# The sample's keys and values in two buffers each, its steps and heads re-spaced, and the output matrix loaded in eight pieces, in a streaming encoder step

## The chip, the cores and the metric

The kernel runs on one core of a Trainium2 chip. The metric is the device time of one execution in microseconds (us), smaller is better. TensorE (PE; PEld is its weight load), VectorE (DVE), ScalarE (ACT) and GpSimd (POOL) compute. SyncE (SP) computes nothing: it issues DMAs and waits. GpSimd issues the indirect DMAs. Each engine works through its own list in order.

## The reference

One layer for a prompt of 1024 tokens and a sample of 32 tokens that has 2048 tokens of cached keys and values. After one joint projection come stick-breaking attention, window attention, the output matrix, and a retrieval network (PEER) that fetches, for each token and each of 8 heads, 16 rows out of 16384.

```python
def stick_breaking(q, k, v, q_pos, k_pos):
    z = jnp.einsum('bqhd,bshd->bhqs', q, k).astype(jnp.float32) * (HEAD_DIM ** -0.5)
    visible = (k_pos[None, :] < q_pos[:, None])[None, None]
    log_keep = jnp.where(visible, jax.nn.log_sigmoid(-z), 0.0)
    between = lax.cumsum(log_keep, axis=3, reverse=True) - log_keep
    a = jnp.where(visible, jnp.exp(jax.nn.log_sigmoid(z) + between), 0.0)
    return jnp.einsum('bhqs,bshd->bqhd', a.astype(v.dtype), v)
...
    merged = jnp.concatenate([rms_norm(o_sb.reshape(b, t, SB_WIDTH), g_sb),
                              rms_norm(o_sw.reshape(b, t, SWA_WIDTH), g_sw)], axis=-1)
    h = x + merged @ w_out
    return h + peer_ffn(rms_norm(h, g_ffn), w_q, keys_1, keys_2, u, v)
...
        # peer_ffn: scores against two sets of 128 keys, top 16 of each, top 16 of their sums -> ids, gs
        hid = jax.nn.gelu(jnp.einsum('thkd,td->thk', u[ids], xs), approximate=False)
        return jnp.einsum('thk,thkd->td', gs * hid, v[ids])
```

## The kernel before, in words

A first phase projects the first 384 prompt tokens and the sample. The second phase, `fused_phase`, takes nearly all of the time. Its backbone is 1056 **gathers**: `pool.indirect_dma_start` (L895) fetches 128 rows of `peer_uv`, 8 KB each (1.05 MB), into one of 7 buffers `uv`; DVE takes their dot product with the tokens (`dot`, L1112), ACT makes a gelu of it and a diagonal matrix (`experts`, L1033 and L1039), and PE adds the weighted rows up (`experts`, L1627, two gathers at a time). A buffer is free again after that matmul: POOL waits for it (`vmm`) before the gather 7 places on.

All engines run the same loop over **slots** n; slot n has gather n. Everything else is hung on slots by hand, through functions that give a slot number; engines run ahead of one another as far as semaphores let them. There are 8 prompt tiles t of 128 tokens, and the sample is t = 8 (`NT`). For each, in order:

- **steps** (`step_slot`): 2 to 16 of them for a prompt tile, 17 for the sample, each over 128 keys. For a step at slot n, SP loads keys (`load_k`) and values (`load_v`), PE makes `scores` at n into `z`, ACT `softplus` at n + 1, DVE `keep` at n + 3, PE `sums` at n + 4, ACT `weights` at n + 6, PE `values` at n + 8. Steps of prompt tiles stand 4 slots apart and have two buffers for keys and two for values; the sample's stand 5 apart (slots 822 to 902), with one buffer each. So `load_k` of a sample step holds for the scores of the step ahead, and `load_v` for its values.
- the window (four slots, 4 apart), the tail (norms, output matrix, residual), and
- eight **heads** (`route_slot`), at slot n: PE makes `queries` (L1564) in slots n and n + 1, DVE cuts the scores at n + 9 (`first_eight`, whose L1239 frees the bank that the next head's queries wait for, `cut`), and the row numbers are there at n + 18. Heads stand 11 slots apart in tile 1, 14 or 15 in tiles 2 to 7, and 9 in the sample (slots 961 to 1024).

ACT's `log_table()` loads the table set for exp and ln before `softplus` and before `weights` where the last set was another; the gelu in `experts`, which runs in odd slots, loads its own again. The output matrix `w_out` (4.2 MB) for tiles 3 to 8 goes into the space of the late projection's buffers: `load_w_out` (L812) issues four DMAs of 1 MB at slot 222, ahead of the first keys of tile 3, whose first step is at slot 229.

## Time and profile before

| | |
|---|---|
| median of 3 runs | 3384.24 us (3364.96 to 3384.81) |
| the profiled execution's own time | 3389.14 us |
| its span, first to last instruction | 3387.3 us |
| busy: PE, DVE, ACT, POOL | 2562.7, 2221.3, 1388.7, 1601.4 us |
| mean granted clock of PE | 0.882 of full |
| read from HBM | 1201.97 MB |

The span leaves out 1.8 us of the execution's own time, and the profiled execution took 4.9 us more than the median run. The DMA share of a stretch is the busy time of the 16 DMA engines' packets over that of the stretch; where packets of two queues overlap it reads slightly above 1.

### The profile page before, as it was taken

How to read it: one execution, taken by the hardware profiler on the slowest of the kernel's cores; microseconds unless marked ns; L12 is line 12 of the kernel's file. 1: busy time of each engine (PE TensorE's matmuls, PEld its weight loads, DVE VectorE, ACT ScalarE, POOL GpSimd, SP SyncE). 2: the span in 40 equal slices, each digit the busy share in tenths (PEclk: the TensorE clock that was granted, in tenths of full speed). 3: DMA queues.
4: the chain of work that ended last, by engine and by line, in shares of the span. 5: the costliest groups of instructions: out<-in, count | busy, mean ns of one | idle time of the engine just before them, and what ended most of it. 6: DMA issues, size and time to landing. Idle time of an engine off the chain costs nothing.

```text
span 3387.3 us, 38329 instructions
## 1 busy us (share of the span) xinstructions
PE 2562.7 (76%) x10637; PEld 1201.1 (35%) x10637; DVE 2221.3 (66%) x5640; ACT 1388.7 (41%) x3224; POOL 1601.4 (47%) x1634
## 2 busy tenths in 40 slices
PE   7898787877858676877787768876887777767664
PEld 4464333433324322432343224332343234322321
DVE  2037746785657857776777666777777666675775
ACT  2124522652226424652365335544565344442222
POOL 1104444443535555555555544555554554456443
PEclk9899889988979888979799889888998888888777
DMA  6538899999989999999999999999999999999887
GB/s 213 175 97 327 329 407 416 375 381 349 421 354 391 380 381 401 371 381 396 381 387 363 383 397 357 378 384 406 363 395 387 406 391 383 377 393 390 354 355 291
DMA packets 246919, 1225.21 MB, mean 362 GB/s; under 512 B 30721, under 2 KB 90801, under 8 KB 110513
## 3 DMA queue, kind: packets, MB, share of 16 engines
q0 software_dynamic: 154208, 1112.07, 82.3%
q1 hardware_dynamic: 92496, 110.69, 10.0%
q8 instruction: 85, 1.39, 0.2%
q14 instruction: 130, 1.06, 0.1%
HBM read 1201.97 MB, written 20.79 MB: 361 GB/s over the span
## 4 chain that ended last, share of the span: by engine, by line
PE 37%; DMA 26%; DVE 10%; issue 7%; ACT 6%; POOL 5%; DVEq 2%; ACTq 1%; SPq 1%; POOLq 0%
DMA f_uv<-peer_uv,f_idx 18%; PE f_y_acc L1627 17%; PE f_q_ps L1564 5%; DVE f_uv L1112 4%; DMA f_work<-cache_sb_kT 4%; POOL f_uv L895 3%; PE f_z L1523 3%; PE f_z L1390 2%; DMA f_work<-scratch_projT 2%; ACT f_diag L1039 2%; ACT L1033 2%; PE f_z L1371 2%; POOL f_gate_fold L883 1%; PE f_z L1397 1%; PE f_o_sb L1416 1%
## 5 line engine op out<-in xcount | busy, mean ns | idle before, releaser
L895 POOL DMA_INDIRECT f_uv<-peer_uv,f_idx x1056 | 1244.9, 1179 | 1625.9 <-PE f_y_acc L1627 1338.0
L1112 DVE CUSTOM_DVE_ANT_0 f_uv<-f_uv,f_x_rep 128x1024 f32<-128x1024 f32 x1056 | 1304.0, 1238 | 779.7 <-DMA f_uv<-peer_uv,f_idx 777.1
L1627 PE MATMUL f_y_acc<-f_uv,f_diag 128*64 128x512 f32 x4224 | 1249.9, 712 | 578.6 <-ACT f_diag L1039 562.1
L1627 PEld LDWEIGHTS f_y_acc<-f_uv,f_diag 128*64 128x64 f32 x4224 | 300.1, 154 | 1198.1 <-ACT f_diag L1039 726.0
L1033 ACT ACTIVATE f_act_hid<-f_hid 128x2 f32<-128x2 f32 x528 | 107.2, 203 | 1272.7 <-DVE f_hid L1112 1270.5
L1564 PE MATMUL f_q_ps<-r_w_q,f_xnT 128*128 128x256 f32 x1152 | 311.1, 421 | 55.1 <-DVE f_cut L1239 55.1
L883 POOL TENSOR_TENSOR f_gate_fold<-r_fold,f_gates 128x128 f32<-128x128 f32 x528 | 328.6, 622 | 9.7
L1039 ACT ACTIVATE f_diag<-f_gate_fold,f_act_hid 128x64 f32<-128x64 f32 x1056 | 310.3, 340 | 37.9 <-issue 1.1
L1564 PEld LDWEIGHTS f_q_ps<-r_w_q,f_xnT 128*128 128x128 f32 x1152 | 233.2, 210 | 141.3 <-DVE f_cut L1239 65.2
L1033 ACT ACT_TABLE_LOAD x196 | 251.5, 1283 | 3.5
L908 ACT ACT_TABLE_LOAD x119 | 152.7, 1283 | 240.7 <-PE f_z L1371 189.7
L1390 PE MATMUL f_z<-f_work,r_neg_suffix 128*128 128x512 f32 (+2 forms) x178 | 105.1, 676 | 10.5 <-DVE f_work L1134 5.9
L367 PE MATMUL proj<-xnT,w_cols 128*128 128x416 f32 x288 | 106.4, 526 | 2.7 <-DVE xnT L332 2.7
L1523 PE MATMUL f_z<-r_w_out,f_work 128*128 128x512 f32 (+1 forms) x192 | 93.9, 625 | 10.2 <-DVE f_work L1199 10.2
L1371 PE MATMUL f_z<-f_q_pad,f_work 128*128 128x256 f32 x288 | 79.6, 401 | 28.3 <-DMA f_work<-scratch_projT 28.3
L1416 PEld LDWEIGHTS f_o_sb<-f_work 128*128 128x128 f32 (+2 forms) x848 | 91.4, 166 | 26.0 <-issue 21.2
L1134 DVE SCALAR_TENSOR_TENSOR f_work<-f_z,f_work 128x512 f32<-128x512 f32 (+2 forms) x89 | 56.9, 640 | 54.1 <-ACT f_work L929 49.1
L1416 PE MATMUL f_o_sb<-f_work 128*128 128x64 f32 (+2 forms) x848 | 91.6, 255 | 0.4 <-DMA f_work<-cache_sb_v 0.2
L1112 DVE DVE_READ_ACCUMULATOR2_ANT f_hid<- 128x1 f32 x1056 | 85.7, 81 | 0.0
L1371 PEld LDWEIGHTS f_z<-f_q_pad,f_work 128*128 128x128 f32 x288 | 57.1, 201 | 72.7 <-issue 67.9
L1491 PE MATMUL f_o_sb<-r_w_out 128*128 128x256 f32 (+1 forms) x224 | 72.6, 444 | 0.0
L367 PEld LDWEIGHTS proj<-xnT,w_cols 128*128 128x128 f32 x288 | 55.2, 196 | 46.4 <-issue 43.1
(184 smaller groups left out, 2747.1 us busy)
## 6 DMA issues: line engine op xcount, KB each, us to landing
f_uv<-peer_uv,f_idx POOLq DMA_INDIRECT x1056, 9.5
f_work<-scratch_projT SPq DMA_DIRECT2D x86, 128.0 KB
w_cols<-w_blocks SPq DMA_DIRECT2D x18, 512.0 KB, 3.9
r_w_out<-w_blocks SPq DMA_DIRECT2D x36, 256.0 KB, 7.2
f_work<-out_sb_v_prompt SPq DMA_DIRECT2D x72, 128.0 KB, 7.3
r_w_q<-w_peer_q SPq DMA_DIRECT2D x8, 1024.0 KB, 7.5
x_in<-x_prompt SPq DMA_DIRECT2D x8, 512.0 KB, 4.6
f_q_pad<-scratch_projT SPq DMA_DIRECT2D x64, 64.0 KB
```

The lines of the kernel that those rows point to most:

```text
L367: last = nc.tensor.matmul(acc[c % 2][:, 0:EARLY + TS], w[:, c % 2, k, :], xnT[:, k, :], start=(k == 0), stop=(k == DK - 1))
L883: nc.gpsimd.tensor_tensor(gate_fold[:, batch % 4, :, :], fold[:].unsqueeze(1).broadcast_to(full), gates[:, t % 2, head, k:k + 2].unsqueeze ...
L895: pool.indirect_dma_start(uv[:, n % RING, :], None, io["peer_uv"], bass.IndirectOffsetOnAxis(ap=idx[:, t % 2, head, k:k + 1], axis=0),).th ...
L1033: nc.scalar.activation(act_hid[:, batch % 4, :], hid[:, batch % 8, :], ACT.Gelu)
L1039: made = nc.scalar.activation(diag[:, batch % 3, i, :], gate_fold[:, batch % 4, i, :], ACT.Copy, scale=act_hid[:, batch % 4, i:i + 1])
L1112: nc.vector.tensor_tensor_reduce(row_u, row_u, x_rep[:, g % 2, :], 1.0, 0.0, ALU.mult, ALU.add, hid[:, n // 2 % 8, n % 2:n % 2 + 1]).then_ ...
L1371: last = nc.tensor.matmul(z[:, at:at + 256], kT[:, (e % 2) * 256 + m * P:(e % 2) * 256 + (m + 1) * P], q_pad[:, f, m, :, :].rearrange("p a ...
L1390: nc.tensor.matmul(out, neg_suffix[0:keys, 0:keys], sp[0:keys, 0:width], start=False, stop=False, skip_group_check=True)
L1416: last = nc.tensor.matmul(o_sb[0:n, hd * HD:(hd + 1) * HD], probs[0:keys, i * n:(i + 1) * n], v_blk[0:keys, col:col + HD], start=(e == 0 a ...
L1523: last = nc.tensor.matmul(z[0:rows, b * 512:(b + 1) * 512], mergedT[:, k, 0:rows], w[:, b * 512:(b + 1) * 512], start=(k == 0), stop=(k == ...
L1564: last = nc.tensor.matmul(q_ps[:, 0:2 * QH], xnT[:, k, :], w_q[:, k, head * 2 * QH:(head + 1) * 2 * QH], start=(k == 0), stop=(k == DK - 1))
L1627: last = nc.tensor.matmul(y_acc[i * GT:(i + 1) * GT, b * 512:(b + 1) * 512], diag[:, batch % 3, i, :], uv[:, n % RING, DM + b * 512:DM + ( ...
```

## The change

The sample's steps stand 4 slots apart in place of 5: they still begin at slot 822 and end at 886 in place of 902. Its window moves from slot 913 to 896, its tail from 933 to 916, and its heads stand 11 slots apart, at 944 to 1021 in place of 961 to 1024. Keys and values of odd steps get second buffers, `k_odd` and `v_odd`, in halves of attention buffers that the sample's narrower steps leave free; each lies there in two runs of 1 KB a partition. The cached keys are laid out in memory so that a partition's 512 numbers are one run of 2 KB, where they were four of 512 B. The output matrix is loaded in eight pieces of 0.5 MB, one every 4 slots from slot 225 on. `load_k` and `load_v` of the sample now stand at the prompt's places in SP's list, and `load_window` of the sample also holds for the values of step 15, since `vw` shares its space with `v_odd`.

```diff
@@ -439,7 +439,7 @@
         return t * P - 69 + 14 * head
-    return t * P - 77 + 15 * head if t < NT else t * P - 63 + 9 * head
+    return t * P - 77 + 15 * head if t < NT else t * P - 80 + 11 * head
...
 def stretch(t):
@@ -459,7 +459,7 @@
 def step_slot(t, e):
...
-    return window_slot(t, 0) - 6 - (4 if t < NT else 5) * (steps_of(t) - e)
+    return window_slot(t, 0) - 6 - 4 * (steps_of(t) - e)
@@ -503,6 +503,8 @@
         vw = work[:, 5 * 512 + 2 * P:6 * 512].rearrange("p (b c) -> p b c", b=2)
+        k_odd = part(1, 3).rearrange("p (a c) -> p a c", a=2)[:, :, 256:512]
+        v_odd = part(2, 6).rearrange("p (a c) -> p a c", a=2)[:, :, 768:1024]
         merged = part(0, 2)
@@ -580,9 +582,7 @@
         def half_loads(t, e):
...
-            if t < NT:
-                return STEP0[t] // 2 + e // 2 + 1
-            return STEP0[NT] // 2 + e + 1
+            return STEP0[t] // 2 + e // 2 + 1
...
         def first_key(t):
@@ -685,28 +685,36 @@
             def load_k(t, e):
                 s, f, b = step(t, e)
-                if e >= 2 or (e and t == NT):
-                    hold(sync, S["z"], s - 1 if t < NT else s)
+                if e >= 2:
+                    hold(sync, S["z"], s - 1)
                 elif t:
                     hold(sync, S["xn"], t)
+                    if t == NT and e == 1:
+                        hold(sync, S["tx"], t)
+                        hold(sync, S["h_out"], t * 16)
                 if t < NT:
...
                 else:
-                    every = kT.rearrange("p (c t) -> p c t", c=4)
-                    src = (io["projT"][4:8, :, SEQ:TOK] if b == 0
-                           else io["cache_sb_kT"][:, :, PAST - b * P:PAST - b * P + P])
-                    sync.dma_start(every[:, :, 0:keys_of(t, b)], src.rearrange("c p t -> p c t")).then_inc(S_K[0], 16)
+                    if b == 0:
+                        dst = kT.rearrange("p (c t) -> p c t", c=4)[:, :, 0:TS]
+                        src = io["projT"][4:8, :, SEQ:TOK].rearrange("c p t -> p c t")
+                    else:
+                        dst = k_odd if e % 2 else kT.rearrange("p (a c) -> p a c", a=2)
+                        src = io["cache_sb_kT"][PAST // P - b].rearrange("p (a c) -> p a c", a=2)
+                    sync.dma_start(dst, src).then_inc(S_K[e % 2], 16)
...
             def load_v(t, e):
                 s, f, b = step(t, e)
-                if e >= 2 or (e and t == NT):
-                    hold(sync, S["pv"], s - 1 if t < NT else s)
+                if e >= 2:
+                    hold(sync, S["pv"], s - 1)
                 elif t:
...
                     hold(sync, S["h_out"], t * 16)
+                    if t == NT and e == 1:
+                        hold(sync, S["tx"], t)
                 if t < NT:
@@ -714,7 +722,9 @@
                 else:
-                    sync.dma_start(v_blk, io["cache_sb_v"][PAST - b * P:PAST - b * P + P, :]).then_inc(S_V[0], 16)
+                    sync.dma_start(v_odd if e % 2 else v_blk.rearrange("p (a c) -> p a c", a=2),
+                                   io["cache_sb_v"][PAST - b * P:PAST - b * P + P, :].rearrange("p (a c) -> p a c", a=2)
+                                   ).then_inc(S_V[e % 2], 16)
...
             def load_kw(t):
@@ -732,6 +742,8 @@
             def load_window(t):
                 hold(sync, S["tri"], STEP0[t + 1])
+                if t == NT:
+                    hold(sync, S["pv"], STEP0[NT] + steps_of(NT) - 1)
                 if t < NT:
@@ -814,13 +826,9 @@
                     load_step_q(at[0])
-                if (at := STEP_AT.get(n + 6)) and at[0] < NT:
+                if (at := STEP_AT.get(n + 6)):
                     load_k(*at)
-                if (at := STEP_AT.get(n + 3)) and at[0] == NT:
-                    load_k(*at)
-                if (at := STEP_AT.get(n)) and at[0] < NT:
-                    load_v(*at)
-                if (at := STEP_AT.get(n - 4)) and at[0] == NT:
+                if (at := STEP_AT.get(n)):
                     load_v(*at)
@@ -859,11 +867,13 @@
                     load_w_out(w_first, "w_first")
-                if n == LATE_SLOT[-1] + 11:
+                if n == LATE_SLOT[-1] + 14:
                     for s in range(2):
...
                         hold(sync, S_LNS[s], all_nat_stores(s) * 16)
-                    load_w_out(w_out, "w_out")
+                for k in range(DK):
+                    if n == LATE_SLOT[-1] + 14 + 4 * k:
+                        sync.dma_start(w_out[:, k, :], io["w_out"][k * P:(k + 1) * P, :]).then_inc(S["w_out"], 16)
             for dst, src in copies:
@@ -1374,10 +1384,11 @@
                         pe.wait_ge(S_Q[f], 64 * t + 32)
-                    pe.wait_ge(S_K[0], half_loads(t, e) * 16)
+                    pe.wait_ge(S_K[e % 2], half_loads(t, e) * 16)
                     for m in range(4):
                         at = (e % 2) * 512 + m * 2 * TS
-                        last = nc.tensor.matmul(z[0:keys, at:at + 2 * TS], kT[:, m * P:m * P + keys],
+                        block = k_odd[:, m // 2, m % 2 * P:m % 2 * P + keys] if e % 2 else kT[:, m * P:m * P + keys]
+                        last = nc.tensor.matmul(z[0:keys, at:at + 2 * TS], block,
                                                 q_pad[:, m // 2, m % 2, :, 0:TS], start=(m == 0), stop=False,
@@ -1406,15 +1417,15 @@
                     pe.wait_ge(S["late_ev"], evicted(step_slot(t, 0) + 8))
-                if t < NT:
-                    pe.wait_ge(S_V[e % 2], half_loads(t, e) * 16)
-                else:
-                    pe.wait_ge(S_V[0], half_loads(t, e) * 16)
+                pe.wait_ge(S_V[e % 2], half_loads(t, e) * 16)
                 for i in range(4 if t < NT else NH):
...
                     col = (e % 2) * 256 + i * HD if t < NT else i * HD
+                    block = v_blk[0:keys, col:col + HD]
+                    if t == NT and e % 2:
+                        block = v_odd[0:keys, col // 256, col % 256:col % 256 + HD]
                     last = nc.tensor.matmul(o_sb[0:n, hd * HD:(hd + 1) * HD], probs[0:keys, i * n:(i + 1) * n],
-                                            v_blk[0:keys, col:col + HD], start=(e == 0 and i == 0), stop=False,
+                                            block, start=(e == 0 and i == 0), stop=False,
                                             skip_group_check=True)
@@ -1517,7 +1528,7 @@
                     if k == 0:
-                        pe.wait_ge(S["w_out" if t else "w_first"], 64)
+                        pe.wait_ge(S["w_out" if t else "w_first"], DK * 16 if t else 64)
                     w = (w_out if t else w_first)[:, k, :]
@@ -1698,8 +1709,8 @@
     arrays["w_blocks"] = np.ascontiguousarray(blocks)
-    keys = arrays["cache_sb_k"].reshape(PAST, 4, P)
-    arrays["cache_sb_kT"] = np.ascontiguousarray(keys.transpose(1, 2, 0))
+    keys = arrays["cache_sb_k"].reshape(PAST // P, P, 4, P)
+    arrays["cache_sb_kT"] = np.ascontiguousarray(keys.transpose(0, 3, 2, 1)).reshape(PAST // P, P, 4 * P)
     keys = arrays["cache_swa_k"].reshape(WIN, 2, HD)```

SyncE's DMAs around the output matrix and the first keys of tile 3, before (L694 loads keys, L712 values, L668 queries):

```order
L783 DMA scratch_projT<-r_w_out 128x256
L812 DMA r_w_out<-w_out 128x2x1024 x4
L668 DMA f_q_pad<-scratch_projT 64x2x128 x4
L694 DMA f_work<-scratch_projT 128x2x128 x2
L712 DMA f_work<-out_sb_v_prompt 128x256
```

And now (L697 keys, L720 values, L876 the matrix):

```order
L795 DMA scratch_projT<-r_w_out 128x256
L668 DMA f_q_pad<-scratch_projT 64x2x128 x4
L697 DMA f_work<-scratch_projT 128x2x128
L876 DMA r_w_out<-w_out 128x1024
L697 DMA f_work<-scratch_projT 128x2x128
L720 DMA f_work<-out_sb_v_prompt 128x256
L876 DMA r_w_out<-w_out 128x1024
L697 DMA f_work<-scratch_projT 128x2x128
```

The queries, the keys and the values of tile 3's first steps stand ahead of or between the pieces of the matrix, where all of it stood ahead of them.

ScalarE in one sample step before (L940 is `weights`, L925 to L929 `softplus`, L1033 and L1039 the gelu and the diagonals of `experts`):

```order
L1017 ACTIVATE f_q<-f_q_ps 128x256
L908 ACT_TABLE_LOAD
L940 ACTIVATE f_work<-f_z 128x256
L925 ACTIVATE f_work<-f_z 128x256
L927 ACTIVATE f_work<-f_work 128x256
L929 ACTIVATE f_work<-f_work 128x256
L1033 ACT_TABLE_LOAD
L1033 ACTIVATE f_act_hid<-f_hid 128x2
L1039 ACTIVATE f_diag<-f_gate_fold,f_act_hid 128x64 x2
L1023 ACTIVATE f_qT<-f_q_ps 128x256
L1033 ACTIVATE f_act_hid<-f_hid 128x2
L1039 ACTIVATE f_diag<-f_gate_fold,f_act_hid 128x64 x2
```

And now, a little over one step (L950 `weights`, L935 to L939 `softplus`, L1043 and L1049 `experts`):

```order
L1043 ACT_TABLE_LOAD
L1043 ACTIVATE f_act_hid<-f_hid 128x2
L1049 ACTIVATE f_diag<-f_gate_fold,f_act_hid 128x64 x2
L918 ACT_TABLE_LOAD
L950 ACTIVATE f_work<-f_z 128x256
L1043 ACT_TABLE_LOAD
L1043 ACTIVATE f_act_hid<-f_hid 128x2
L1049 ACTIVATE f_diag<-f_gate_fold,f_act_hid 128x64 x2
L918 ACT_TABLE_LOAD
L935 ACTIVATE f_work<-f_z 128x256
L937 ACTIVATE f_work<-f_work 128x256
L939 ACTIVATE f_work<-f_work 128x256
```

`weights` and `softplus` stood in one slot; they are now in two slots with an `experts` between, so that a step of 4 slots has four table loads, where one of 5 slots had two. In the whole list the table loads go from 399 to 426.

TensorE between two heads of the sample before (L1564 queries, L1572 and L1578 turns and key scores, L1600 the selection, L1627 `experts`, 4 matmuls for two gathers):

```order
L1564 MATMUL f_q_ps<-r_w_q,f_xnT 128x256 x8
L1627 MATMUL f_y_acc<-f_uv,f_diag 64x512 x8
L1572 MATMUL f_q_ps<-r_ident,f_q 128x128 x2
L1627 MATMUL f_y_acc<-f_uv,f_diag 64x512 x4
L1578 MATMUL f_q_ps<-r_keysT,f_qT 128x128 x2
L1600 MATMUL f_sel_ps<-f_packed,r_ident 32x8 x4
L1627 MATMUL f_y_acc<-f_uv,f_diag 64x512 x4
L1564 MATMUL f_q_ps<-r_w_q,f_xnT 128x256 x4
```

And now (L1575 queries, L1638 `experts`):

```order
L1575 MATMUL f_q_ps<-r_w_q,f_xnT 128x256 x8
L1638 MATMUL f_y_acc<-f_uv,f_diag 64x512 x8
L1583 MATMUL f_q_ps<-r_ident,f_q 128x128 x2
L1611 MATMUL f_sel_ps<-f_packed,r_ident 32x8 x4
L1638 MATMUL f_y_acc<-f_uv,f_diag 64x512 x4
L1589 MATMUL f_q_ps<-r_keysT,f_qT 128x128 x2
L1638 MATMUL f_y_acc<-f_uv,f_diag 64x512 x8
L1575 MATMUL f_q_ps<-r_w_q,f_xnT 128x256 x4
```

Between the queries of two heads stand five pairs of gathers where there were four.

## Rows read from the trace of the kernel before

**Rows 1.** The page: the gathers' DMA queue: packets, MB, share of 16 engines

```profile
q0 software_dynamic: 154208, 1112.07, 82.3%
```

**Rows 2.** The page: the chain that ended last, by engine

```profile
PE 37%; DMA 26%; DVE 10%; issue 7%; ACT 6%; POOL 5%; DVEq 2%; ACTq 1%; SPq 1%; POOLq 0%
```

**Rows 3.** Stretch, us, L1112's busy time and instructions, clock, DMA share, GB/s

```profile
953.20:1011.30 58.10, 17.38 (x29) 0.74 0.84 325
1011.30:1068.20 56.90, 24.83 (x40) 0.97 1.02 402
531.60:583.80 52.20, 23.57 (x39) 0.97 1.02 413
2349.50:2536.40 186.90, 79.34 (x128) 0.94 0.99 382
1997.90:2167.80 169.90, 68.97 (x113) 0.90 0.96 370
2611.50:2685.60 74.10, 34.72 (x56) 0.88 1.00 409
2693.20:2951.90 258.70, 107.03 (x172) 0.86 0.97 383
3050.30:3118.40 68.10, 32.52 (x53) 0.90 1.01 412
3118.40:3310.00 191.60, 79.19 (x129) 0.77 0.89 355
```

**Rows 4.** DMA issues of SyncE in time, 940 to 970 us

```profile
943.70 2.19 SPq L812 DMA_DIRECT2D r_w_out<-w_out  x4
...
958.28 10.24 SPq L694 DMA_DIRECT2D f_work<-scratch_projT  x2
```

**Rows 5.** The chain in time, from 950 us on: start, us, what

```profile
958.28 35.59 DMA f_work<-scratch_projT
```

**Rows 6.** DMA queue of SyncE's transfers, 953.2 to 1011.3 us

```profile
q1 hardware_dynamic: 2567, 4.26, 20.0%
```

**Rows 7.** The chain in time, inside the sample's steps

```profile
2799.82 9.65 DMA f_work<-cache_sb_kT
...
2809.61 1.09 PE f_z L1380 x8
...
2810.76 14.22 DMA f_work<-cache_sb_kT
...
2826.26 16.03 DMA f_work<-cache_sb_kT
```

**Rows 8.** SyncE's queue and issues, 2693.2 to 2951.9 us; last: us to landing

```profile
q1 hardware_dynamic: 11982, 8.70, 10.8%
...
f_work<-cache_sb_v SPq DMA_DIRECT2D x16, 256.0 KB, 8.4
...
f_work<-cache_swa_v SPq DMA_DIRECT2D x1, 64.0 KB, 9.8
```

**Rows 9.** ScalarE's table loads, 2693.2 to 2951.9 us

```profile
L1033 ACT ACT_TABLE_LOAD x20 | 25.7, 1283 | 0.4
...
L908 ACT ACT_TABLE_LOAD x18 | 23.1, 1283 | 1.5 <-PE f_z L1397 0.8 <-PE f_z L1380 0.4
```

**Rows 10.** ScalarE in time, a load and what follows it

```profile
2784.80 1.28 ACT L1033 ACT_TABLE_LOAD   x1
2786.10 0.20 ACT L1033 ACTIVATE f_act_hid<-f_hid 128x2 f32<-128x2 f32 x1
```

**Rows 11.** Waits, 3118.4 to 3310 us: total, times, longest

```profile
PE f_q_ps L1564 <- DVE f_cut L1239: 35.0, 7, 7.8
```

**Rows 12.** The chain in time, one head of the sample

```profile
3162.16 9.20 DMA f_uv<-peer_uv,f_idx
...
3174.44 3.78 PE f_q_ps L1564 x8
...
3188.46 10.25 DMA f_uv<-peer_uv,f_idx
```

## Prediction

> **What bounds the kernel now.** I read the page's DMA queues first. The gathers' queue alone fills 82.3% of the 16 DMA engines' span [rows 1]: 1056 gathers of 1.05 MB. The chain that ended last is spread over PE 37%, DMA 26% and DVE 10% [rows 2], which is what a ring of 7 buffers looks like: each gather waits for a matmul, each matmul for a gather. So the question for every stretch is whether the DMA engines are full. If they are, nothing but bytes and packets counts; if not, something holds the ring up.
>
> The table of stretches answers it. L1112 runs two instructions a slot, so half its count is the number of slots. Where only heads and gathers run, 28 slots took 74.10 us at a share of 1.00: 2.65 us a slot, which I use as the full-DMA pace. 19 slots of tile 1, with heads 11 apart, took 52.20 us at 1.02 (2.75; it also carries projection weights). Step stretches of prompt tiles, with steps 4 apart, are at 2.92 (64 slots, 0.99) and 3.03 (56 slots, 0.96) [rows 3]. Three stretches have idle DMA engines, and the change touches each of them [rows 3]:
> - 953.2 to 1011.3, slots 222 to 236: share 0.84 and 4.15 us a slot;
> - 2693.2 to 2951.9, the sample's steps, 86 slots: 0.97 and 3.01;
> - 3118.4 to 3310.0, the sample's heads 1 to 7, 64 slots: 0.89 and 2.99.
>
> The idle time there is 9.3, 7.8 and 21.1 us, 38 us in all. That is the stock from which the change can draw, apart from cheaper packets.
>
> **A, the output matrix in pieces.** Four 1 MB loads are issued at 943.7; the first keys of tile 3 are issued at 958.3, behind them in SP's queue [rows 4], and PE waits 35.59 us for those keys [rows 5]. PE is in order, so the matmuls of gathers stand behind the scores, the ring runs dry and the DMA engines idle. Now the queries and keys go first, and each piece has 4 slots (10.6 us) to itself. SyncE's queue was busy for 20.0% of 58.1 us, 11.6 us, with 4.26 MB [rows 6]; nearly all of that is the matrix, and it has to be paid in either order. What can go is the idle 9.3 us; the slots right behind (1011.3 to 1068.2) are full, at 1.02 [rows 3], and give nothing. A step stretch of a prompt tile keeps 1 to 4% idle, so 1 to 2 us stay: **−8 us**, bounds −9 and −4. The last piece is issued at slot 253 and is wanted at 296, 43 slots or over 110 us later: no new wait. The pieces pass SP's holds for keys and values, so they may bunch by two, no more.
>
> **B, the sample's steps.** Here the chain is a closed loop: matmul of the scores 1.09 us, then a wait for the next keys of 9.65, 14.22 or 16.03 us, since the load may only go out when the scores have used the one buffer [rows 7]. One turn takes about 258.7/17 = 15.2 us for 5 slots, where the full pace would be 13.3 plus this stretch's other transfers. With two buffers, `load_k` goes out 8 slots of PE ahead of its use (over 21 us), and values the same. Values landed in a median of 8.4 us [rows 8], so the wait goes. What is late next is the DMA queue itself, which is already at 0.97: the gain is at most 7.8 us of idle, whatever the chain says.
>
> Packets: SyncE's queue was busy 10.8% of 258.7, 27.9 us, for 8.70 MB [rows 8], or 3.2 us a MB, with half of the 8.4 MB of cache in runs of 512 B; the matrix, in 4 KB runs, went at 11.6/4.26 = 2.7 [rows 6]. Keys now come in 2 KB runs (even steps) or 1 KB (odd). If values go at 2.7, the keys and the rest now cost (27.9 − 4.2 × 2.7)/4.5 = 3.7; at about 3.0 they save 4.2 × 0.7 = 3 us. Values of odd steps go from 2 KB to 1 KB runs, which gives back a few tenths.
>
> Against this stand denser steps. If 68 slots ran at the prompt's 2.92, and carried 4.3 MB more than prompt steps (two pieces of 262 KB a step, not 131) at 3.2 us a MB, that is 198.6 + 13.8, and 18 more slots at 2.65 give 47.7: 260.1 us, +1.4. With the dearer prompt stretch, 3.03, it is 267.6, +9. With all idle time gone and packets saved it is −11. The sample's matmuls and activations are half as wide as the prompt's, so I take a value nearer to the good end: **−5 us**, bounds −11 and +9.
>
> ScalarE pays for it. A step had two table loads and now has four, 27 more in all. In this stretch 20 and 18 loads of 1283 ns took 48.8 us [rows 9]; 27 more add 34.6 us of ACT. Half of the new ones lie ahead of a gelu that a gather waits for. I cost them at nothing in the sum, because ACT often waits for the dot product before its gelu, and the load is done while it waits; and because a delay of 1.28 us in a ring of 7 slots (18.5 us) only shortens the queue at the DMA engines, it does not drain it. If that cover is thin, it is the rival below. The next activation starts 0.02 us after the load ends [rows 10].
>
> The Trainium skill (ScalarE: Activation LUTs, What ACT_TABLE_LOAD costs) gives a switch 1283 ns plus some 1380 ns of drain, 2.66 us in all. By that the 27 would be 72 us of ACT, an estimate from that page; the 0.02 us of [rows 10] does not agree with the drain, and the sum goes by the row.
>
> The new hold in `load_window` costs nothing: values of step 15 are made in the same slot, 890, as the sums for which it held already, and the window's DVE work is 7 slots on, where its last loads land in 9.8 us [rows 8].
>
> **C, heads 11 slots apart.** At 9 apart, the queries of a head wait in PE for the cut of the head before, which DVE makes in that very slot, behind the dot product of its gather. PE thus waits for the newest gather although its own matmuls are of older ones: 7 waits, 35.0 us [rows 11]. The chain shows one turn: gather 9.20 us, a short piece of DVE, queries 3.78 us, `experts`, then the next gather, at 3162.16 and again at 3188.46 [rows 12]: 26.3 us for 9 slots, where the full pace is 23.9. At 11 apart the cut is made 2 slots before it is wanted. Tile 1 has that spacing, and its stretch runs at a share of 1.02 [rows 3]. Heads now cover slots 944 to 1021. These 90 slots, 944 to 1033, took 68.1 + 191.6 = 259.7 us [rows 3]; at 2.65 they take 238.5, −21. Some of the idle time has other sources (the copies of x at slot 1000, the output of tile 7 from 1024 on), for which I keep 2: **−19 us**. The weak end: PE's clock was 0.77 in the stretch [rows 3], and a head's eight first matmuls of queries took 3.78 us [rows 12]; if PE itself held the ring, half of the loss would stay, −10. The strong end is −22.
>
> **The sum**: −8 − 5 − 19 = −32. The profiled execution goes from 3389.1 to 3357 us. It was 4.9 us above the median; from the median 3384.2 this is **3352 us**, a ratio of 0.9905.
>
> **Rivals.**
> 1. *Everything idle goes*: A −9, B −11, C −22 = −42, 3342 us. For it: full shares in the stretches without the waits. Against: every step stretch has 1 to 4% idle.
> 2. *One spacing is still too tight*: either PE's half clock holds the ring in the heads (C −10), or four-slot steps cost as much as tile 6's (B +9 with C −19). That gives −8 − 5 − 10 = −23 or −8 + 9 − 19 = −18: about 3364 us. For it: 0.77, and 3.03 us a slot. Against: tile 1.
> 3. *Slower: table loads.* If ACT's lead over PE in the sample's steps is less than a load, each of the 27 loads is passed on to the ring: 34.6 us more than idle −3 for packets, with A and C as forecast: −8 − 19 − 3 + 34.6 = +5, 3389 us. It decides once over 27 of the 34.6 us are exposed. For it: both of two `experts` now have a load ahead. Against: the prompt's steps have one load per two `experts` before a gelu, with activations twice as wide, and stay at 0.96 to 0.99. By the page's price, 72 us, it would be 3426 us; the row of 0.02 us speaks against that.
> 4. *The change does not do what it says*: the idle time in these stretches comes from the ring as such, and reappears elsewhere, with A alone left: −8, 3376 us. For it: the medians spread over 20 us without any change. Against: the three waits are named in the trace, and one of them is 35.59 us long.
>
> **How the numbers follow.** Forecast (−26 to −38) 0.45; rival 1 0.22; rival 2 0.18; rival 3 0.08; rival 4 0.07. The range leaves out rivals 3 and 4 and a little of the others, and adds some us at either end for the spread of runs: 3334 to 3374. One per cent, about what can be told from no change, is 34 us, right beside the forecast: over 1% faster means under 3350.4. That is rival 1 and a little under half of the forecast: 0.42. Over 1% slower needs the table loads at more than the row's price, the page's for instance: 0.04. Within 1%: 0.54.
>
> **What the profile after will show.** If A is right, no chain piece of tens of us on `scratch_projT` near slot 229, and a share near 1 there. If B is right, `cache_sb_kT` is gone from the chain, the scores wait for `f_work` at most once or twice, and the steps' 68 slots run at 2.9 to 3.0 us. If C is right, L1564 waits for L1239 in no head of the sample, and the share in the last heads is 0.97 or more. I am wrong if those waits are gone and the stretches are no shorter: then `f_act_hid` or `f_diag` behind table loads would be the releasers named.

## Result and the profile after

The changed kernel takes 3339.64 us in the median of 4 runs (3332.55 to 3345.27), the kernel before in the same comparison 3384.52 us. The ratio is 0.9873, with a 95% interval of 0.9851 to 0.9896: 43 us less, between 35 and 50. Its profiled execution took 3334.36 us, with a span of 3332.6.

The page of the changed kernel: the gathers' queue, and the chain by engine, beside [rows 1] and [rows 2].

```profile
q0 software_dynamic: 154208, 1112.07, 83.6%
...
PE 35%; DMA 23%; DVE 14%; issue 7%; ACT 6%; POOL 5%; DVEq 3%; ACTq 2%; SPq 0%; POOLq 0%
```

The gathers fill a little more of a shorter span, and DMA and PE have each lost some of the chain to DVE. Now the stretches, as in [rows 3] (stretch, us, busy time of the dot product's line, clock, DMA share, GB/s): slots 222 to 236, 236 to 256, 822 to 908, 944 to 970 and 970 to 1034 of the changed kernel.

```profile
946.70:988.60 41.90, 17.58 (x28) 0.88 1.02 408
988.60:1049.50 60.90, 24.87 (x41) 0.97 1.02 410
2669.80:2922.40 252.60, 107.87 (x173) 0.88 1.00 397
3021.60:3090.40 68.80, 32.61 (x52) 0.93 1.01 413
3090.40:3258.70 168.30, 80.98 (x129) 0.81 0.99 399
```

Slots 222 to 236 went from 58.1 us at a share of 0.84 to 41.9 at 1.02; slots 970 to 1034 from 191.6 at 0.89 to 168.3 at 0.99. The sample's steps and what follows them, 822 to 908, went from 258.7 at 0.97 to 252.6 at 1.00.

SyncE's issues at tile 3's first step in the changed kernel, beside [rows 4]:

```profile
938.67 2.56 SPq L668 DMA_DIRECT2D f_q_pad<-scratch_projT  x4
941.33 0.55 SPq L697 DMA_DIRECT2D f_work<-scratch_projT  x1
942.13 0.34 SPq L876 DMA_DIRECT2D r_w_out<-w_out  x1
942.57 0.38 SPq L697 DMA_DIRECT2D f_work<-scratch_projT  x1
943.10 1.19 SPq L720 DMA_DIRECT2D f_work<-out_sb_v_prompt  x1
944.34 2.55 SPq L876 DMA_DIRECT2D r_w_out<-w_out  x1
966.58 0.38 SPq L697 DMA_DIRECT2D f_work<-scratch_projT  x1
```

Queries and two blocks of keys and one of values go out between 938.7 and 944, with the first piece of the matrix between them and the second right behind; then SP holds for the first scores, to 966.6. The first keys took 35.59 us from issue to landing in [rows 5]. PE itself stood still for the last part of that, by the waits of the kernel before, 953.2 to 1068.2 us:

```profile
PE f_z L1371 <- DMA f_work<-scratch_projT: 17.5, 1, 17.5
```

The same row in the changed kernel, 946.7 to 1049.5 us:

```profile
PE f_z L1381 <- DMA f_work<-scratch_projT: 0.5, 1, 0.5
```

The sample's heads, 3021.6 to 3258.7 us, beside the 35.0 us of [rows 11]:

```profile
PE f_q_ps L1575 <- DVE f_cut L1249: 1.3, 1, 1.3
```

And the table loads in slots 822 to 890 of the changed kernel, beside [rows 9]:

```profile
L918 ACT ACT_TABLE_LOAD x33 | 42.3, 1283 | 35.2 <-PE f_z L1391 34.9
L1043 ACT ACT_TABLE_LOAD x33 | 42.3, 1283 | 0.6
```

66 loads in 68 slots, where 38 stood in 86: that is what the order of instructions had shown.

For comparing kernels I cut each trace at the starts of the dot products of the same slots. In us:

| slots | before | after | code of the change there |
|---|---|---|---|
| 0 to 222 | 692.0 | 684.7 | none |
| 222 to 256 | 115.0 | 102.8 | output matrix |
| 256 to 509 | 725.3 | 724.2 | none |
| 509 to 701 | 555.9 | 548.7 | none |
| 701 to 822 | 343.8 | 347.4 | none |
| 822 to 908 | 258.7 | 252.6 | steps, keys, values |
| 908 to 944 | 98.4 | 99.3 | window, tail |
| 944 to 1034 | 259.7 | 237.1 | heads |
| 1034 to the end | 77.3 | 73.9 | last head |

The three touched stretches give −12.2, −6.1 and −22.6, together −41; the other −14 of these two profiles lie mostly where the code is the same. How far such a stretch moves by itself, the later profiles tell: over the fourteen, slots 509 to 701 took 540.8 to 556.7 us; over the twelve with the same heads in tile 0, slots 0 to 222 took 682.5 to 694.6.

### The profile page after: what moved, and what is told of

It is laid out like the page before. It is cut to its first block, busy times and chain, and to the rows that moved or that the text cites. A ratio compares the mean times of both kernels' runs of the same rounds, so it can differ in the third digit from the quotient of the medians.

```text
span 3332.6 us, 38365 instructions
## 1 busy us (share of the span) xinstructions
PE 2533.4 (76%) x10637; PEld 1186.3 (36%) x10637; DVE 2220.2 (67%) x5640; ACT 1422.6 (43%) x3251; POOL 1621.2 (49%) x1634
## 3 DMA queue, kind: packets, MB, share of 16 engines
q0 software_dynamic: 154208, 1112.07, 83.6%
## 4 chain that ended last, share of the span: by engine, by line
PE 35%; DMA 23%; DVE 14%; issue 7%; ACT 6%; POOL 5%; DVEq 3%; ACTq 2%; SPq 0%; POOLq 0%
DMA f_uv<-peer_uv,f_idx 21%; PE f_y_acc L1638 16%; DVE f_uv L1122 6%; PE f_q_ps L1575 4%; POOL f_uv L905 3%; PE f_z L1534 3%; PE f_z L1401 2%; POOL f_gate_fold L893 2%; ACT f_diag L1049 2%; PE f_z L1381 2%; ACT L1043 1%; PE f_o_sb L1427 1%; PE f_z L1408 1%; ACTq L1047 1%; DMA f_work<-w_out 1%
## 5 line engine op out<-in xcount | busy, mean ns | idle before, releaser
L1638 PE MATMUL f_y_acc<-f_uv,f_diag 128*64 128x512 f32 x4224 | 1239.9, 707 | 614.2 <-ACT f_diag L1049 583.0
L1638 PEld LDWEIGHTS f_y_acc<-f_uv,f_diag 128*64 128x64 f32 x4224 | 297.7, 153 | 1240.2 <-ACT f_diag L1049 757.4
L1043 ACT ACTIVATE f_act_hid<-f_hid 128x2 f32<-128x2 f32 x528 | 107.3, 203 | 1241.0 <-DVE f_hid L1122 1238.4
L893 POOL TENSOR_TENSOR f_gate_fold<-r_fold,f_gates 128x128 f32<-128x128 f32 x528 | 345.7, 655 | 9.5
L1049 ACT ACTIVATE f_diag<-f_gate_fold,f_act_hid 128x64 f32<-128x64 f32 x1056 | 310.3, 340 | 37.9 <-issue 1.1
L1575 PE MATMUL f_q_ps<-r_w_q,f_xnT 128*128 128x256 f32 x1152 | 292.4, 401 | 20.9 <-DVE f_cut L1249 20.9
L918 ACT ACT_TABLE_LOAD x136 | 174.5, 1283 | 247.1 <-PE f_z L1381 148.6
L1043 ACT ACT_TABLE_LOAD x211 | 270.7, 1283 | 3.7
L1575 PEld LDWEIGHTS f_q_ps<-r_w_q,f_xnT 128*128 128x128 f32 x1152 | 220.7, 199 | 99.5 <-issue 42.4
L1381 PE MATMUL f_z<-f_q_pad,f_work 128*128 128x256 f32 x288 | 76.6, 389 | 11.0 <-DMA f_work<-scratch_projT 11.0
L1381 PEld LDWEIGHTS f_z<-f_q_pad,f_work 128*128 128x128 f32 x288 | 55.1, 194 | 54.4 <-issue 50.1
L1401 PEld LDWEIGHTS f_z<-f_work,r_neg_suffix 128*128 128x128 f32 (+1 forms) x178 | 29.8, 205 | 119.9 <-issue 51.1
## 6 DMA issues: line engine op xcount, KB each, us to landing
r_w_out<-w_blocks SPq DMA_DIRECT2D x36, 256.0 KB
```

The lines of the kernel that those rows point to most:

```text
L893: nc.gpsimd.tensor_tensor(gate_fold[:, batch % 4, :, :], fold[:].unsqueeze(1).broadcast_to(full), gates[:, t % 2, head, k:k + 2].unsqueeze ...
L918: act.preload_act_table_set("natural_log_exp_and_others")
L1043: nc.scalar.activation(act_hid[:, batch % 4, :], hid[:, batch % 8, :], ACT.Gelu)
L1049: made = nc.scalar.activation(diag[:, batch % 3, i, :], gate_fold[:, batch % 4, i, :], ACT.Copy, scale=act_hid[:, batch % 4, i:i + 1])
L1381: last = nc.tensor.matmul(z[:, at:at + 256], kT[:, (e % 2) * 256 + m * P:(e % 2) * 256 + (m + 1) * P], q_pad[:, f, m, :, :].rearrange("p a ...
L1401: nc.tensor.matmul(out, neg_suffix[0:keys, 0:keys], sp[0:keys, 0:width], start=False, stop=False, skip_group_check=True)
```

## Experiments

**The output matrix alone.** The kernel before, with the last part of the diff and its wait only:

```diff
-                if n == LATE_SLOT[-1] + 11:
+                if n == LATE_SLOT[-1] + 14:
...
-                    load_w_out(w_out, "w_out")
+                for k in range(DK):
+                    if n == LATE_SLOT[-1] + 14 + 4 * k:
+                        sync.dma_start(w_out[:, k, :], io["w_out"][k * P:(k + 1) * P, :]).then_inc(S["w_out"], 16)
```

> The kernel before, with only the output matrix in eight pieces. If order in SyncE's queue was the cause (theory 1), the wait of 35.6 us for tile 3's first keys is gone, slots 222 to 256 take about 103 us where they took 115, and the whole is 10 to 14 us faster, with the sample's part as before (ratio near 0.9965). If the ring itself makes the idle time (theory 2), those slots get shorter but slots 256 to 500 give it back, and the whole stays within 4 us.

Measured: ratio 0.9974 (0.9953 to 0.9995), 9 us less. Slots 222 to 256 took 102.6 us. Its stretches 222 to 236, 236 to 256 and 822 to 908:

```profile
954.40:996.40 42.00, 17.74 (x29) 0.87 1.02 407
996.40:1057.00 60.60, 25.38 (x40) 0.92 1.02 410
2676.80:2928.10 251.30, 106.55 (x173) 0.88 1.00 394
```

The first two are those of the changed kernel, and nothing is given back at once: slots 256 to 509 took 725.9 us, before 725.3. Theory 1 holds. The whole came out 9 us faster, just under the 10 to 14 I had expected, with an interval of 2 to 16. The last row has the old step code, and yet took 251.3 us where the kernel before had 258.7: a first warning of how much that stretch varies.

**The matrix behind the first keys, but all at once:**

```diff
-                    if n == LATE_SLOT[-1] + 14 + 4 * k:
+                    if n == LATE_SLOT[-1] + 14:
```

> The changed kernel with all eight pieces of the output matrix at once, but still behind the queries and first keys of tile 3. If it is the order in the queue that counts (theory 1), TensorE does not wait for the first keys; keys and values of the second and third step, behind 4.2 MB, wait instead, some 20 to 30 us once, and slots 222 to 256 take 108 to 114 us (changed kernel 102.8, before 115.0). If the spreading counts for nothing (theory 2), they take under 105.

Measured (one run): 3351.0 us. The two stretches, 222 to 236 and 236 to 256, and PE's wait for prompt keys in them:

```profile
948.60:995.50 46.90, 17.28 (x29) 0.72 1.02 411
995.50:1063.60 68.10, 24.59 (x40) 0.85 0.90 339
```

```profile
PE f_z L1381 <- DMA f_work<-scratch_projT: 10.8, 1, 10.8
```

The first stretch is now full, at 1.02, and the second idles, at 0.90: the hole has moved from the first step of tile 3 to the next. The keys of that step went out at 957.3, behind all eight pieces, and landed 41.5 us later. Together 115.1 us, as in the two profiles with the old loads (115.0 and 117.7) and a little above what theory 1 had; PE's wait was shorter than the 20 to 30 us expected. So the order alone gives little or nothing. With one piece at a time between the loads of the steps the hole is closed; how many pieces may stand together was not tried.

**Heads of the sample 9 and 10 apart, from slot 944:**

```diff
-    return t * P - 77 + 15 * head if t < NT else t * P - 80 + 11 * head
+    return t * P - 77 + 15 * head if t < NT else t * P - 80 + 9 * head
```

> The changed kernel with the sample's heads 9 slots apart again, but still from slot 944 on (to 1007). If the spacing is the cause (theory 1), TensorE waits for the cut in 7 heads again, some 35 us, and the 90 slots from 944 take 250 to 260 us where the changed kernel has 237: the whole 15 to 22 us slower than the changed kernel. If it was the place of the heads (they ran beside other work of the last slots, theory 2), the 90 slots stay under 242 us.

> The changed kernel with the sample's heads 10 slots apart, from 944 to 1014. At 10 the cut of the head before stands one slot ahead of the queries. If one slot is enough (theory 1), there is no wait or some of under 1 us, and the 90 slots from 944 take 237 to 242 us. If the loss goes with the density of heads and not with that wait (theory 2), it lies half way between 9 and 11, near 247 us.

Measured: at 9 apart 3361.0 us, ratio to the kernel before 0.9941 (0.9919 to 0.9963), which is 21 us above the changed kernel's median (23 by the ratios, since the two stand in different comparisons). The wait, and slots 944 to 970 and 970 to 1034:

```profile
PE f_q_ps L1575 <- DVE f_cut L1249: 33.4, 7, 7.8
```

```profile
3018.40:3094.10 75.70, 32.04 (x52) 0.83 0.91 360
3094.10:3277.30 183.20, 79.36 (x128) 0.79 0.92 367
```

The 90 slots took 258.9 us, as before the change (259.7), with the same 7 waits of 33.4 us. It is the spacing, not the place. At 10 apart (one run, 3340.1 us):

```profile
PE f_q_ps L1575 <- DVE f_cut L1249: 18.4, 7, 3.8
```

```profile
3021.50:3094.70 73.20, 32.69 (x53) 0.83 0.93 373
3094.70:3263.20 168.50, 80.51 (x128) 0.83 0.99 399
```

Here PE still waits for the cut in all 7 heads, 18.4 us, against what I had written; but the 90 slots took 241.7, 4.6 above the changed kernel's 237.1. The nine profiles at 11 apart lie between 229.8 and 237.1, with a mean of 233.9, so that waits of 2.6 us each cost 5 to 12 us and waits of 4.8 us 22 to 29. By the means the loss falls faster than the waits (8 of 25 us, with 18.4 of 33.4 us of waits), but there is one profile at each of 9 and 10.

**Keys held back as with one buffer:**

```diff
                 if e >= 2:
-                    hold(sync, S["z"], s - 1)
+                    hold(sync, S["z"], s - 1 if t < NT else s)
```

> The changed kernel, whose sample keys keep their two buffers but are held back as with one: a load goes out only when the scores of the step ahead are done. One turn of that loop was 15.2 us, and there are 17, now 4 slots apart. If the loop was a real bound that full DMA engines only hid (theory 1), the steps' 68 slots take at least 15 x 15.2 = 228 us and up to 258, where they take 200: 25 to 55 us slower than the changed kernel. If the DMA engines take up any such wait (theory 2), under 10 us.

Measured: 3342.8 us, ratio 0.9882 (0.9850 to 0.9914), which can't be told from the changed kernel. Slots 822 to 890, and the wait for keys:

```profile
2677.50:2880.50 203.00, 84.59 (x137) 0.88 0.99 390
```

```profile
PE f_z L1391 <- DMA f_work<-cache_sb_kT: 0.2, 1, 0.2
```

Theory 1 fell. The loads wait for the scores again, and nobody waits for the loads. So the second buffer was not needed to remove the loop. What else had changed was the layout of the keys, hence the next two.

**Keys in runs of 512 B, with two buffers, and held back as well.** The array is laid out as before the change, and a block is loaded in two DMAs:

```diff
-                        dst = k_odd if e % 2 else kT.rearrange("p (a c) -> p a c", a=2)
-                        src = io["cache_sb_kT"][PAST // P - b].rearrange("p (a c) -> p a c", a=2)
+                        half = k_odd if e % 2 else kT.rearrange("p (a c) -> p a c", a=2)
+                        every = io["cache_sb_kT"][:, :, PAST - b * P:PAST - b * P + P].rearrange("c p t -> p c t")
+                        sync.dma_start(half[:, 0, :].rearrange("p (c t) -> p c t", c=2), every[:, 0:2, :]).then_inc(S_K[e % 2], 16)
+                        dst, src = half[:, 1, :].rearrange("p (c t) -> p c t", c=2), every[:, 2:4, :]
```

> The changed kernel with the cached keys in runs of 512 B again, each step's in two DMAs, in their two buffers. My estimate was that long runs save 3 us in the sample's steps: then their 68 slots take 203 us, where the changed kernel has 200.2. If runs do not matter once there are two buffers (theory 2), 200 to 201.

> As the run with runs of 512 B, and each load of keys also held for the scores of the step ahead. With 2 KB runs that hold cost next to nothing: 203.0 us for the 68 slots. If that is because long runs land within the 4 slots (11.8 us) and short ones, which took 10 to 16 us, do not (theory 1), scores now wait for keys in most steps and the 68 slots take 235 to 260 us. If a hold costs nothing because the ring covers it (theory 2), under 208.

Measured without the hold (one run): 3349.5 us, slots 822 to 890 in 201.7 us, which is inside the spread and tells nothing. The queue does tell: SyncE's transfers in these slots, first with runs of 512 B, then in the changed kernel (packets, MB, share).

```profile
q1 hardware_dynamic: 12443, 8.33, 13.1%
```

```profile
q1 hardware_dynamic: 7387, 8.34, 11.8%
```

13.1% of 201.7 against 11.8% of 200.1 us: 26.4 and 23.6 us for the same bytes, 2.8 us from the length of the runs. The waits of this profile have no row of scores waiting for keys: with two buffers short runs are in time. With the hold (one run, 3345.3 us):

```profile
2660.30:2883.00 222.70, 84.66 (x136) 0.83 0.93 358
```

```profile
PE f_z L1393 <- DMA f_work<-cache_sb_kT: 17.4, 7, 4.5
```

222.7 us for the 68 slots, where all ten other profiles with steps 4 apart have 200 to 209, with a share of 0.93. The wait is back, 7 times. This is below the 235 to 260 that theory 1 gave, since I had counted every step at the slowest landings, but no other kernel comes near it. Either a second buffer or long runs remove the wait; only with neither is it there.

The time from issue to landing shows it directly. First short runs, from the kernel with nothing but the output matrix changed (slots 822 to 908), then long ones, from the changed kernel with the keys held back (slots 822 to 890); the last figure is the median in us:

```profile
f_work<-cache_sb_kT SPq DMA_DIRECT2D x15, 256.0 KB, 12.3
```

```profile
f_work<-cache_sb_kT SPq DMA_DIRECT2D x15, 256.0 KB, 7.6
```

The short ones spread from 6.5 to 16.1 us, the long ones from 7.4 to 8.5, though the second trace has a landing for only 8 of its 16 loads. Long runs without the hold took a median of 10.7 and 10.8 us in the two profiles that have landings for them, so the length of the runs is not all that sets this time.

**Long runs alone**, in the kernel before:

```diff
-                    src = (io["projT"][4:8, :, SEQ:TOK] if b == 0
-                           else io["cache_sb_kT"][:, :, PAST - b * P:PAST - b * P + P])
...
+                        dst, src = kT, io["cache_sb_kT"][PAST // P - b]
```

> The kernel before, one buffer and steps 5 apart, with only the cached keys laid out in runs of 2 KB. If it was the landing of short runs that made the loop (theory 1), scores wait for cached keys for under 5 us in all, where they waited 28.7, and slots 822 to 908 take about 252 us where they took 258.6. If the single buffer makes the loop (theory 2), the wait stays above 20 us and the stretch above 256.

Measured (one run): 3365.9 us. The wait for keys in the kernel before, 2693.2 to 2951.9 us:

```profile
PE f_z L1380 <- DMA f_work<-cache_sb_kT: 28.7, 10, 7.0
```

Slots 822 to 908 with long runs alone, and the wait now:

```profile
2687.50:2934.80 247.30, 107.10 (x173) 0.89 1.00 404
```

```profile
PE f_z L1382 <- DMA f_work<-cache_sb_kT: 0.9, 1, 0.9
```

With one buffer and steps 5 apart the stretch is full and took 247.3 us, less than in any kernel with two buffers and steps 4 apart (252.6 and more).

**Two more table loads a step**, 34 in all, behind each of the sample's `weights`:

```diff
                 if (at := STEP_AT.get(n - 6)):
                     weights(*at)
+                    if at[0] == NT:
+                        act.preload_act_table_set("gelu_and_others")
+                        act.preload_act_table_set("natural_log_exp_and_others")
```

> The changed kernel with two more table loads in every step of the sample, 34 more of 1283 ns, 43.6 us of ScalarE, so six a step. If ScalarE's load has cover (theory 1, what the forecast assumed), the 68 slots take 200 to 208 us. If loads are passed on to the ring (theory 2), up to 244. At 96 loads in some 200 us ScalarE would be busy over 80 per cent, so a few us are likely even by theory 1.

Measured (one run): 3352.7 us. ScalarE's loads in slots 822 to 890, and the stretch:

```profile
L918 ACT ACT_TABLE_LOAD x33 | 42.3, 1283 | 10.9 <-PE f_z L1394 10.4
L1043 ACT ACT_TABLE_LOAD x32 | 41.1, 1283 | 0.5
...
L1093 ACT ACT_TABLE_LOAD x16 | 20.5, 1283 | 0.3
L1094 ACT ACT_TABLE_LOAD x16 | 20.5, 1283 | 0.1
```

```profile
2684.80:2890.80 206.00, 84.75 (x137) 0.88 0.99 388
```

That is 97 loads where the changed kernel had 66, 31 more or 39.8 us. ScalarE is busy for 183.5 of 206.0 us (145.3 of 200.1 in the changed kernel), and the stretch took 206.0 us, inside the spread of the same code without them. Against the fastest profile of that code 6 of the 40 us reach the end, against the slowest (208.9) none: theory 1.

**The changed kernel again, and two edits on top of it.** The first moves the sample's `weights` a slot forward into that of the next `softplus` (400 table loads in the list, not 426); the second spaces the heads of tile 0.

```diff
-        return 8 * head - 25
+        return 10 * head - 39
...
-                if (at := STEP_AT.get(n - 6)):
+                if (at := STEP_AT.get(n - 6)) and at[0] < NT:
+                    weights(*at)
+                if (at := STEP_AT.get(n - 5)) and at[0] == NT:
                     weights(*at)
```

> The changed kernel once more, in the same chip's runs as the next one: 3335 to 3348 us, and a ratio to the kernel before of 0.985 to 0.990 by either theory.

> The changed kernel with two further edits. The sample's weights move one slot forward, into the slot of the next step's softplus, so that a step has two table loads in place of four: with full DMA engines (theory 1) this gives under 2 us, slots 822 to 890 still take 198 to 201 us; if loads cost something after all (theory 2), 190 to 196. And the heads of tile 0, which stood 8 apart and of which five waited 17.1 us for the cut, stand 10 apart, from slot -39: slots 0 to 48 should come down from 161 us to 148 to 152 (share 0.90 now), against which the first phase gets 14 slots longer before slot 0, that is 0 to 20 us. Theory 1 expects the whole within 6 us of the changed kernel; theory 2, that heads cost wherever they stand, expects it 5 to 20 us slower.

Measured in one comparison: the changed kernel 3347.3 us, ratio 0.9894 (0.9847 to 0.9940); with both edits 3319.3 us, ratio 0.9839 (0.9785 to 0.9893), its profiled execution at 3318.4. Neither theory had this: the two edits together are worth 28 us by the medians and 19 by the ratios, where theory 1 allowed 6 and theory 2 expected a loss. The changed kernel's own slots 822 to 908 in this profile:

```profile
2676.60:2942.00 265.40, 107.40 (x173) 0.84 0.96 379
```

265.4 us, where the first profile of the same code had 252.6. Slots 822 to 890 of it took 208.9 us, and 208.7 with `weights` moved: fewer table loads give nothing that this stretch can show. The second edit alone:

> The combined kernel without the move of the sample's weights: the changed kernel with the heads of tile 0 10 apart alone. If the move counts for nothing (theory 1), this is within 5 us of the combined kernel, 3314 to 3330 us, with slots 0 to 48 at 136 to 142 us and the time to slot 0 at 270. If the move was worth something that the spread of the step stretch hid (theory 2), it is over 8 us slower.

Measured in another comparison: 3329.1 us, ratio 0.9853 (0.9829 to 0.9878). That is slower than the combined kernel by 10 us in the medians and 5 in the ratios, with overlapping intervals, so the totals neither meet nor exclude theory 2. The stretch itself gives it no support: slots 822 to 890 took 203.3 us here, with 66 table loads before `softplus`, `weights` and the gelu, and 208.7 in the combined kernel, with 36. Slots 0 to 48 and the wait for the cut up to 420 us; then slots 0 to 48 of the changed kernel and the wait from 262 to 423 us (19.6 us in 7 waits up to 420):

```profile
270.70:407.80 137.10, 59.14 (x96) 0.98 0.94 358
```

```profile
PE f_q_ps L1575 <- DVE f_cut L1249: 3.3, 2, 1.8
```

```profile
262.00:423.00 161.00, 60.10 (x97) 0.90 0.90 344
```

```profile
PE f_q_ps L1575 <- DVE f_cut L1249: 17.1, 5, 5.2
```

24 us less in 48 slots (137.1 and, in the combined kernel, 138.2, against 159.5 to 167.3 in the others), for 8.7 us more ahead of slot 0 (270.7, from 262.0). For the first figure I had expected 9 to 13. The net of 15 us agrees with the ratios of this kernel and of the changed one in its second comparison, which are 14 us apart.

## Why the prediction was right, and where it was not

The time is inside the range, 3334 to 3374, 12 us under the forecast; the forecast's −32 is a little short of the interval's near end, −35. The likeliest case's own band had ended at −38, and rival 1 (−42) came closest in number, though not by its own terms. Of the three outcomes with a chance, within one per cent had 0.54 and over one per cent faster 0.42; it is the second. The signs named for the profile came true but for one wait of 1.3 us for the cut, where none was to be left; the steps' 68 slots run at 2.94 us.

**A** was forecast at −8, bounds −9 and −4, and measured −12.2 and, by the kernel with nothing else, −12.4, beyond its strong bound. The mechanism is as told, except that "PE waits 35.59 us" is a misreading: that is the time to landing, and PE idled for 17.5 of it. The size failed at the step that took a share of 1.00 for full: slots 236 to 256 were at 1.02 in both kernels, and so is the mended stretch. At 1.02 the 58.1 us at 0.84 would have taken 47.8, which is 10.3 less, not 9.3. And the 1 to 2 us kept for what a step stretch leaves idle were not needed. The other 2 us are less busy time of the DMA engines in slots 222 to 256, share times length: 106.8 us before and 104.9 after. No run tells why. That pieces "may bunch by two, no more" is what the issues show, and the burst shows why it matters.

**B** was forecast at −5, bounds −11 and +9. The one pair of profiles gave −6.1. Over all, the old step code took 258.7 and 251.3 us, the new 252.6, 254.0, 255.2, 256.7, 256.7 and 265.4 (the six kernels that leave its steps as they are): nothing that can be told from zero, nor from the forecast. It is the same when counted to slot 944, so that the window and the tail, which moved forward, are in: 357.1 and 349.6 us with the old steps, 351.9 to 363.6 in those six, and 344.5 with long runs alone. The step that failed is the cause: "with two buffers ... so the wait goes". A second buffer is enough for that, as the kernel with short runs and two buffers shows, but it was not needed: the wait went with the long runs alone, and did not come back when the loads were held as with one buffer. The prediction had priced the runs by the queue's busy time only, and not by when a load lands. The limit was right, the chain's 28.7 us of waits hid behind DMA engines at 0.97, and so was the 3 us for the packets (2.8). What steps 4 apart give or cost over 5 apart with long runs is not settled: the one profile with both took 247.3 us, 4 under the old layout at 5 apart and 5 under the shortest at 4 apart, in a stretch where the same code spreads over 13.

**Table loads** at nothing: held. 31 further ones cost at most 6 us, and with 30 fewer in slots 822 to 890 the stretch was no shorter, so no run supports rival 3. By the row of 1.283 us ScalarE's busy time should rise by 39.8, and it rose by 38.2, from 145.3 to 183.5 us in a stretch of 206.0. The Trainium skill (ScalarE: Activation LUTs, What ACT_TABLE_LOAD costs) has 1283 ns for the load itself, with which the trace agrees, and 2.66 us for a switch with its drain. 31 at that price, an estimate from that page, would be 82 us more, and 145 + 82 does not fit in 206: here too the measurement disagrees.

**The new hold in `load_window`** at nothing: slots 890 to 944 took 151.7 us, before 156.3, where the last three steps still stood in them. No run takes the hold out by itself.

**C** was forecast at −19, bounds −22 and −10, and measured −22.6, just past its strong end; with the other eight profiles at 11 apart (229.8 to 235.4) against the three of the old code (256.8 to 259.7) it is nearer −25. The cause was tested directly: 9 apart in the new place has the old time and the old waits. The mis-sized term is the 2 us kept for the copies of x and the output of tile 7, and the pace of 2.65: the stretch runs at 2.63 a slot throughout. Rival 2's half of the loss did not stay, with the clock at 0.81 in slots 970 to 1034, after 0.77.

**Rival 4** had all idle time but A's reappear elsewhere. It did not, in A or in C.

**The sum.** −12 for A, −23 to −25 for C and about 0 for B is −35 to −37. That the forecast of −32 lies so near is partly luck: A and C were put 8 to 10 us too low together, and B 5 too high. The first comparison gave −43 (−50 to −35), the second, of the same code, −36 (−52 to −20).

## What to carry to other kernels

Where a ring of transfers feeds everything, ask of each stretch whether the DMA engines are full, read "full" from a neighbouring stretch, and spend effort only on those that fall below: here two holes, with 30 us of idle time by the share, gave the 35 to 37 us, while 28.7 us of waits in a stretch at 0.97 were worth next to nothing. A load that a step waits for must not stand behind a burst, and moving it ahead by one step moves the hole by one step; spreading the burst closes it. Before doubling a buffer, look at how long the load takes to land: four times longer runs alone removed the same wait.

## What was not expected of the hardware

- The DMA share of a full stretch with two busy queues read 1.02 (slots 222 to 256), with hardly anything beside the gathers 0.99 to 1.01 (the heads).
- With the gathers' 8 KB rows in the other queue, 256 KB in runs of 512 B landed 6.5 to 16.1 us after issue, each load held for the scores of the step ahead; in runs of 2 KB, held in the same way, 7.4 to 8.5 us (8 of 16 loads). The long ones, with 4 slots to land in (under 12 us), were late once, by 0.2 us. The queue's busy time for all of the sample's loads differed by 2.8 us in 68 slots only. The length of runs mattered to when a load lands far more than to what it costs.
- PE's waits are hidden in part: 7 of 2.6 us on average went with 5 to 12 us more in 90 slots, 7 of 4.8 us with 22 to 29.
- ScalarE was busy for 89% of a stretch (183.5 of 206.0 us) with little or no loss.
- Stretches of the same code differ by up to 13 us in 250 (822 to 908) and 16 in 550 (509 to 701) from one profile to the next.
